# Streaming-encoder block on one core: two token blocks share each weight piece, V rows gathered by token, 128x32 column tiles, causal attention, one unrolled timetable

## What is computed

```
h = RMSNorm(x); [q|k|v|xc|B|C] = h @ W_in          # 1024 x 3072
sb = StickBreaking(QKNorm(q), QKNorm(k), v)         # 8 heads of 64, strictly causal:
     # A[t,s] = sigmoid(z_ts) * prod_{s<j<t} (1 - sigmoid(z_tj)),  s < t
cv = B * causal_depthwise_conv3(C * xc)             # 512 channels
x = x + concat(RMSNorm(sb), RMSNorm(cv)) @ W_out
h2 = RMSNorm(x); q = h2 @ peer_w_q                  # 8 heads of 2 x 128
     # per head: top 16 of 128 keys twice, their 256 sums, top 16 of these, softmax gate
x = x + sum over 8 x 16 experts of gate * gelu(u[idx] . h2) * v[idx]
```

## Time and profile before

| | |
|---|---|
| time, median of 3 | 3484.75 us (3473.43 to 3490.35) |
| span of the profiled execution | 3468.2 us |
| TensorE / VectorE / ScalarE / GpSimd busy | 85% / 64% / 24% / 66% |
| DMA | 1286.74 MB, mean 371 GB/s |
| of it gathers / weights and the rest | 1073.87 MB / 210.41 MB |
| granted TensorE clock, mean | 0.923 |

### The profile page before, as it was taken

One profiled execution on the slowest core, in us unless ns is written; L12 is line 12 of the kernel. 1 busy time (PEld: TensorE's weight loads), 2 busy tenths in 40 slices (PEclk: granted clock), 3 DMA queues, 4 the chain that ended last, 5 costly groups with the idle time before them and its releaser, 6 DMA issues.

```text
span 3468.2 us, 35295 instructions
## 1 busy us (share of the span) xinstructions
PE 2935.7 (85%) x10472; PEld 1601.8 (46%) x10472; DVE 2204.2 (64%) x5172; ACT 834.0 (24%) x1771; POOL 2280.0 (66%) x2133
## 2 busy tenths in 40 slices
PE   7479987899859997699976999769997699977777
PEld 5436452465525654256532556326563364633333
DVE  3656677465865758557595576846678566774444
ACT  1024211252113411134111341113411143111111
POOL 1256767667676666766667676776767766677775
PEclk9789998999979999899998999889998899988988
DMA  6689999999999999999999999999999999999998
GB/s 210 228 318 387 361 409 371 378 377 376 409 369 382 366 386 408 357 388 349 408 402 353 410 346 409 384 355 409 352 409 382 365 405 354 409 347 397 393 394 328
DMA packets 353146, 1286.74 MB, mean 371 GB/s; under 512 B 39344, under 2 KB 39472, under 8 KB 352944
## 3 DMA queue, kind: packets, MB, share of 16 engines
q0 software_dynamic: 294912, 1073.87, 80.4%
q1 hardware_dynamic: 58032, 210.41, 15.7%
HBM read 1279.93 MB, written 4.19 MB: 370 GB/s over the span
## 4 chain that ended last, share of the span: by engine, by line
PE 53%; DVE 16%; POOL 14%; issue 13%; DMA 2%; ACT 1%; POOLq 0%; DVEq 0%; ACTq 0%; SPq 0%
PE acc L512 27%; PE pm L395 14%; POOL v_ring L342 7%; POOL u_ring L349 7%; DVE u_ring L924 5%; PE pz L395 3%; PE pz L416 3%; PE pm L428 3%; DMA u_ring<-table_u,idx_now 2%; PE pt L401 2%; ACT diag L612 1%; DVE top_i L749 1%; DVE rc L741 1%; DVE top_i L739 1%; DVE ra L770 1%
## 5 line engine op out<-in xcount | busy, mean ns | idle before, releaser
L512 PE MATMUL acc<-v_ring,diag 128*128 128x512 f32 x4096 | 1939.6, 630 | 499.9 <-ACT diag L612 499.9
L924 DVE CUSTOM_DVE_ANT_0 u_ring<-u_ring,h_mix 128x1024 f32<-128x1024 f32 x1024 | 1220.5, 1223 | 539.0 <-DMA u_ring<-table_u,idx_now 526.3
L512 PEld LDWEIGHTS acc<-v_ring,diag 128*128 128x128 f32 x4096 | 812.1, 203 | 1537.9 <-issue 1236.0
L349 POOL DMA_INDIRECT u_ring<-table_u,idx_now x1024 | 1097.7, 1072 | 588.0 <-issue 313.3
L342 POOL DMA_INDIRECT v_ring<-table_v,idx_now x1024 | 1151.2, 1124 | 447.3 <-issue 350.6
L612 ACT ACTIVATE diag<-ident,wgt 128x128 f32<-128x128 f32 x1024 | 327.0, 390 | 657.9 <-DVE wgt L915 657.9
L395 PEld LDWEIGHTS pm<-hT,w_ring 128*128 128x128 f32 x3584 | 412.0, 193 | 48.0 <-issue 46.8
L395 PE MATMUL pm<-hT,w_ring 128*128 128x128 f32 x3584 | 420.9, 278 | 2.0 <-issue 1.2
L617 ACT ACTIVATE acts<-dots 128x4 f32<-128x4 f32 x256 | 52.5, 205 | 1083.3 <-DVE dots L924 1082.6
L722 DVE TENSOR_TENSOR_SCAN ra<-rc 128x1024 f32<-128x1024 f32 (+1 forms) x64 | 130.9, 2054 | 64.1 <-ACT rc L580 64.1
L712 DVE TENSOR_TENSOR ra<-pz,band 128x1024 f32<-128x1024 f32 x56 | 68.6, 1225 | 160.4 <-PE pz L416 160.0
(11 more groups left out here) (118 smaller groups left out, 1635.9 us busy)
## 6 DMA issues: line engine op xcount, KB each, us to landing
w_ring<-wstream SPq DMA_DIRECT2D x384, 512.0 KB, 7.6
v_ring<-table_v,idx_now POOLq DMA_INDIRECT x1024, 9.5
u_ring<-table_u,idx_now POOLq DMA_INDIRECT x1024, 9.2
rb<-x_in_dram SPq DMA_DIRECT2D x8, 512.0 KB, 6.8
y_out_dram<-x_mix SPq DMA_DIRECT2D x8, 512.0 KB, 7.3
g_all<-norm SPq DMA_DIRECT2D x1, 512.0 KB, 7.6
keysT<-keys SPq DMA_DIRECT2D x1, 128.0 KB, 6.9
chan_sb<-chan SPq DMA_DIRECT2D x1, 15.0 KB, 7.1
```

Source lines behind the costliest of these rows:

```text
L349: nc.gpsimd.indirect_dma_start(out=u_ring[:, j % U_SLOTS, :], out_offset=None, in_=peer_u, in_offset=bass.IndirectOffsetOnAxis(ap=idx_now[ ...
L512: mm = nc.tensor.matmul(acc[:, half * 512:(half + 1) * 512], diag[:, n % 2, j, :], v_ring[:, k % V_SLOTS, half * 512:(half + 1) * 512], st ...
L924: d = V.tensor_tensor_reduce(u, u, h_mix[:], 1.0, 0.0, ALU.mult, ALU.add, dots[:, n % 2, j:j + 1])
```

## The change

- **Shared pieces.** Fronts run for blocks 0, 1, (2,3), (4,5) and (6,7). In a front of two, each piece in `w_ring` multiplies both blocks, so 5 x 48 pieces are loaded in place of 8 x 48. x is kept in 5 slots, h2, indices and gates in 4.
- **V by token.** The indices of a quarter are turned on TensorE (`spread_out`) into a second table, `idx_v`, in which one gather of 128 rows holds 32 picks of 4 tokens. The 32 weights per token are turned the same way and placed once per quarter into `wmask` (`weigh`, `place`), whose columns are zero except for those 4 tokens. A group of 4 such gathers is summed with 128x32 stationaries, each into its own 32 PSUM partitions. ScalarE's diagonals go. V has 8 slots instead of 16 and lags 9 groups behind U.
- **Causal attention.** Block b uses keys 0 to 128(b+1). Blocks 0 to 7 take 8, 4, 2, 2, 1, 1, 1, 1 heads at a time. The mask is added on TensorE, as ident times band into the same PSUM.
- **Timetable.** All engines are unrolled. A tick is one pick of one block (1024 in all); `WHEN` gives for each front the ticks between which its steps are spread by their lengths. The first front's main part stands before tick 0; after tick 852 there is no front work.
- Small ones: the second norm's factor is applied after the product with the keys; gates are normed per quarter; the convolution goes channel group by channel group; GpSimd reads its indices straight from the tables.

```
+SUPER = (1, 1, 2, 2, 2)
+WHEN = [(-1, 1, 9, 17, 25), (26, 94, 102, 110, 118), (118, 246, 272, 298, 324), (326, 500, 532, 564, 596),
+        (600, 756, 788, 820, 852)]
...
+    piece = 2.2 * n
...
+            attend += [(4.0, ("scores", b, p)), (6.0, ("stick", b, p)), (3.0, ("turn", b, p)),
+                       (2.0, ("values", b, p))]
...
+        section += [(piece, ("w", PIECE_PEER + 4 * q + c)) for c in range(4)]
+        section += [(3.0, ("key_scores", q))]
+        for b in blocks:
+            section += [(9.0, ("rank", b, q)), (7.0, ("combine", b, q)), (8.0, ("look_up", b, q)),
+                        (3.0, ("turn_picks", b, q))]
...
+            def gather_u(s):
...
+                wait(pool, dots_done, s + 1 - U_SLOTS // GROUP)
...
+            def gather_v(g):
...
+                wait(pool, group_done, g + 1 - V_SLOTS // GROUP)
+                for i in range(GROUP):
+                    slot, c = (g * GROUP + i) % V_SLOTS, q * QPICKS + i * QGROUPS + j
...
+            for s in range(BLOCKS * GROUPS + V_LAG):
+                if s >= V_LAG:
+                    gather_v(s - V_LAG)
+                if s < BLOCKS * GROUPS:
+                    gather_u(s)
...
+            def spread_out(dst, src):
+                every = ident[:].rearrange("p (c a) -> p a c", a=4)
+                for a in range(4):
+                    mm = nc.tensor.matmul(dst[32 * a:32 * a + 32, :], src[:], every[:, a, :], start=True, stop=True)
...
+            def mix(g):
...
+                for half in range(2):
+                    for i in range(GROUP):
+                        t = g * GROUP + i
...
+                        mm = nc.tensor.matmul(acc[32 * i:32 * i + 32, half * 512:(half + 1) * 512],
+                                              wmask[:, quarter % 2, i, 32 * j:32 * j + 32],
+                                              v_ring[:, t % V_SLOTS, half * 512:(half + 1) * 512],
+                                              start=(g % GROUPS == 0), stop=(g % GROUPS == GROUPS - 1))
...
+            def stick(b, p):
+                dve.wait_ge(beta_ready, PASS0[b] + p + 1)
+                n = P * (b + 1)
+                for h, o in heads_of(b, p):
+                    back = rc[:, o:o + n][:, ::-1]
+                    step(V.tensor_tensor_scan(back, back, back, 1.0, ALU.mult, ALU.bypass))
...
+            for k in range(-1, END):
+                for s in STEPS.get(k, ()):
...
+                    front(*s)
+                if 0 <= k < TICKS:
+                    dot(k)
+                quarter = k // QPICKS - 1
+                if 0 <= quarter < BLOCKS * QUARTERS:
+                    if k % QPICKS == 1:
+                        weigh(quarter)
+                    if k % QPICKS == 3:
...
+                        place(quarter)
```

More of the change, by code:

```diff
@@ new lines, in timetable @@
+def timetable():
+    out = {}
+    for f in range(len(SUPER)):
+        for section, (a, z) in zip(front_steps(f), zip(WHEN[f], WHEN[f][1:])):
+            total, so_far = sum(length for length, _ in section), 0.0
+            for length, step in section:
+                tick = -1 if a < 0 else a + int((z - a) * so_far / total)
+                out.setdefault(tick, []).append((f, *step))
+                so_far += length
+    return out
+STEPS = timetable()
+TICKS = BLOCKS * PICKS
+END = TICKS + GROUP * (V_LAG + 2)
@@ L287, in _ @@
             sp.dma_start(g2_all[:], norm2_g.to_broadcast([P, D])).then_inc(consts_in, 16)
[L288 to L297, removed]
+            for k in range(-1, END):
+                for step in STEPS.get(k, ()):
+                    front(*step)
+                for b in range(BLOCKS):
+                    if k == finish_tick(b):
+                        store(b)
+            for b in range(BLOCKS - X_SLOTS, BLOCKS):
+                sp.wait_ge(y_out[b % X_SLOTS], 16 * (b // X_SLOTS + 1))
         @block.gpsimd
@@ new lines, in front, with small_bank @@
+                if name == "turn_picks":
+                    here = picked(*args)
+                    pe.wait_ge(idx_ready, here)
+                    small_bank("picks")
+                    spread_out(pick_cols, idx_f).then_inc(idx_turned, 1)
+            small_uses = {"picks": 0, "weights": 0, "sums": 0}
+            def small_bank(what):
+                wait(pe, idx_kept, small_uses["picks"])
+                wait(pe, wmask_ready, small_uses["weights"])
+                wait(pe, sum_kept, small_uses["sums"])
+                small_uses[what] += 1
@@ new lines, in front @@
+                if name == "gate":
+                    q = args[1]
+                    act.wait_ge(gate_arg, picked(b, q))
+                    g = gates[:, b % STASH, 2 * q:2 * q + 2, :]
+                    nc.scalar.activation(g, g, ACT.Exp).then_inc(gate_exp, 1)
+            act.wait_ge(chan_in, 16)
+            act.wait_ge(ones_set, 1)
+            nc.scalar.activation(acts[:, 0, 0:1], ones[:], ACT.Sigmoid)
+            for k in range(-1, END):
+                quarter = k // QPICKS - 1
+                if k % QPICKS == 0 and 0 <= quarter < BLOCKS * QUARTERS:
+                    act.wait_ge(dots_done, QGROUPS * (quarter + 1))
+                    nc.scalar.activation(acts[:, quarter % 2, :], dots[:, quarter % 2, :],
+                                         ACT.Gelu).then_inc(gelu_done, 1)
+                for step in STEPS.get(k, ()):
+                    front(*step)
```

1276 lines of the change are left out of this document (635 added, 641 removed).

## The result

The changed kernel takes 3337.32 us, median of 4 runs (3331.49 to 3349.26), beside 3482.47 us of the kernel before on the same chip: ratio 0.9584, interval 0.9556 to 0.9611. That is 145 us less. The forecast was 3225 us in a range of 3090 to 3380: the direction and the range held, the gain is 56% of the one forecast. The experiments ran on other chips. On one the kernel before takes 3490 us; on the other two it takes some 3648 and 3615 us, and where gathers alone are in flight the variants move 362 to 369 GB/s there, not 408. Each run is therefore compared by its ratio to the kernel before on its own chip. On the last of these chips only two of seven runs of the kernel before (3593 and 3634 us) were in the fast state, with the others at 3655 to 3681; the ratios there go by these two, hence their wide intervals.

What follows compares the result with a forecast made beforehand. The prediction took DMA plus 7% as the bound, lost where DVE and POOL can't keep the queue full. Stages 241 + 292 + 630 + 802 + 743 + 451 + 50 = 3209 us of span, plus 16.6, gave 3225; range 3090 to 3380.

Steps and rivals of the forecast that it cites:

- ticks 644 to 715: Attention of blocks 6 and 7, without weight pieces: 71 ticks at POOL's 2.78 us each, 197 us.
- the chain of a pass: One attention pass, from stick through turn, copy, values and scores to two sigmoids: about 8 us, against 12.3 to 13.9 in the timetable.
- rival C: Column tiles don't overlap and/or PE runs at 1.2 GHz ("plus 5" on the chain): 3345 us; chance 0.19.
- So the time is DMA plus 7%: Kernel before: a block takes 421 us against 392 of transfers at the ceiling, the rest lost to unfilled queues.
- is not on the path while PE keeps up: Faster mix groups save PE 115 us per block, which only shortens DVE's waits for scores.
- 184 us for 144 transfers: Sharing weight pieces between blocks saves 144 transfers at 1.28 us of DMA each.
- the DMA rate: Sign of being right: some 1210 MB moved at about 380 GB/s.
- B: The old loss of 7.5% above the transfer ceiling stays: 3300 us; chance 0.20.
- D: Slower, as DVE's program order becomes the bound: 3616 us at 160 us of waits per block; chance 0.06.
- The other signs: First gather near 125 us, no index-copy waits, last 172 ticks 2.6 us each, mix group under 4, DVE idle for U.
- A: DMA alone sets the time, 2211 transfers after tick 32 at 1.28 us: 3095 us; chance 0.14.
- E: Sharing moves nothing, as the piece ring paces PE and saved bytes lay in slack: 3480 us; chance 0.03.

Runs made afterwards that it cites:

- e1_order: The changed kernel with the next pass's scores placed ahead of this pass's turn in the timetable; ratio 0.9422 to the kernel before.
- e2_best: e1_order with more ticks for the ranks of the first fronts (blocks 1 to 3); 3265.93 us, ratio 0.936 to the kernel before.
- e1_fill: The changed kernel with three extra unused 384-column TensorE products per attention pass from block 2, second pass on; ratio 0.9551 to the kernel before.
- e2_before_cut: The kernel before, loading only 640 of 1024 columns of each weight piece from block 1 on; ratio 0.9963 to the kernel before.
- e1_twice: The changed kernel with each weight piece of the shared fronts loaded a second time, 143 transfers more; 3651.5 us, ratio 0.9981 to the kernel before.
- e3_halfdots: e2_best with each VectorE dot over 512 of 1024 columns, all gathers kept; 3366.3 us, ratio 0.9301 to the kernel before.
- e3_turn: e2_best with the turn placed directly behind the stick for fronts of two blocks; 3397.2 us, ratio 0.9393 to the kernel before.

## Why the prediction was right, and where it was not

*The stages.* Direction and range held, with 112 us between the forecast and the median. Of the 122 us between forecast and measured span, 73 are ticks 644 to 715, priced at POOL's 2.78 us each. That step failed: the chain of a pass was taken as about 8 us and as fitting under 12.3, and it was priced only in rival C, with a slow mix inside. The 8 was a wrong sum. The prediction's own terms give 5 us on TensorE, 2.29 for the scan and 1.22 for the product behind it, and the copy and two sigmoids take some 1 us each: 11.5, with no room left under 12.3. The low clock, which the forecast left to rival C ("plus 5"), adds the rest in block 7: 16.8 us at 0.50 to 0.60, with the mix beside the scan. In block 6 a mix of 3.64 us also stood in the chain, between values and scores (at 2210 us): 17.0 at 0.60. Moving the next scores out of the chain takes 45 to 47 us off the stretch (e1_order, e2_best), the clock's own rise included. At the old order a pass at 0.99 is 4.6 us shorter than one at 0.51 (e1_fill), but how much of the 73 us is the clock's stays open, since no run had the old order at the high clock throughout.

*The reading of the kernel before.* "So the time is DMA plus 7%" was wrong. It rested on high GB/s in the slices and a ceiling seen in two windows. e2_before_cut took a third of the piece bytes away and gained 0.4%. TensorE was busy in 100.00 of 100 us of a window there (1500 to 1600 us), it held 53% of the page's chain, and half of its mix was worth 3.6 points. I had dismissed PE at 85%: its saving "is not on the path while PE keeps up". It was on the path, at least where pieces flow. The forecast was added up from the stages of the kernel after, so this error did not enter its sum; the reason given for the gain was wrong all the same, and that the sum came out near says nothing for it.

*The bytes.* 184 us for 144 transfers was near the right size, after the change: e1_twice gives 159 on a slower chip, 1.11 us each. In the kernel before, a transfer's worth was 0.09 us (11 us for 126), and with half of the mix gone 0.23 (29 us for 126). So what a byte is worth went with the rest of the kernel, and prices read from the trace of before can't show this. What the rest is worth without sharing was not measured: e1_twice has the bytes back, but crowded into the ticks of the shared fronts, where a front per block would spread them.

*Signs.* Of the signs of being right, the DMA rate missed: 363 GB/s over the span, not 380, and it fell lowest in the attention stretch, where POOL waited 36 us for dots and 34 for mixes; waits for dots there were named as a sign of B or D, but they follow from the chain of attention, in which VectorE stands still. The other signs came.

*Sizes that held.* First gather at 121.1 us (125). DVE busy 2070 (2075). A gather on POOL (1106.1 + 1133.1 + 291.7 + 299.2) / 2048 = 1.38 (1.39). DVE's other idling (3331.3 - 2070.3 - 770.6) / 8 = 61 us a block (60), though 113 us of it fell into 71 ticks. Ticks after 852, 2.57 us (2.62).

*Size that did not.* A mix group 1.92 us at the high clock, not 3.5: four tiles overlap, and weight loads do not stretch it. The sum did not use it.

*Rivals.* C came nearest in time (3345), by its clock and chain; its tiles that do not overlap did not happen. B (3300) also lies near, but its reason, a loss over the ceiling of transfers carried on from before, is not it: transfers were not what held that kernel. A was refuted by the attention stretch, D and E by the result; E's thought, that the bytes saved lay in slack, was right for the kernel before.

## What to carry to other kernels

DMA engines that are busy 96% of the time at 90% of their best rate may still be following another engine: take bytes away before crediting them, and read the chain that ended last. What a saved byte is worth depends on which engine is the limit while it flows (0.09 us a transfer before, 1.11 after), so price it in the kernel that it will flow in. Add up a chain across engines term by term before calling it hidden, at both levels of the clock. In such a chain, compute what does not depend on the last step (here the next scores) before waiting for it.

## What the runs showed of the hardware

- Four 128x32 float32 column tiles run nearly side by side: 16 instructions in 1.92 us against 7.13 at full width, and the order in which they are issued does not matter (1.94).
- The granted clock does not follow busy share: 0.63 with PE busy 187 of 270 us on a mixture of transposes, 64-column and 512-column products, 0.79 with 251 of 439 us in mixes alone; three 384-column products per pass raised it from 0.63 to 0.75.
- Chips differ by 4 to 5% in this kernel: gathers alone move 408 GB/s on one (the change, after tick 852) and 368 on another (e1_order, the same ticks).
- A gather's descriptors take GpSimd longer beside VectorE's work: 0.94 us at 2324.51 in the change with no dot beside it, 1.98 at 2318.69 beside dots in a row. With half as long dots 2048 gathers keep it busy 2041 us (e3_halfdots), not 2267 (e3_turn).
